# Three RMS norms taken off the matmuls' path: six units multiply unnormalised tiles and are scaled in the bank

## The reference, cut to what matters

```python
def rms_norm(x, g):
    return x * lax.rsqrt(jnp.mean(x * x, axis=-1, keepdims=True) + RMS_EPS) * g

def first_block(x, ...):
    h = rms_norm(x, norm_mix_g)
    qa, ka, va, qc, kc, vc, rx, rgate, gates = split(h @ w_in)
    ya = moba_attention(qa, ka, va)                 # 8 heads, softmax
    yb = rg_lru(causal_dwconv(rx, ...)) * gelu(rgate)   # a linear recurrence over the tokens
    yc = diff_attention(qc, kc, vc)                 # 4 heads, each with two softmaxes, then an RMS norm
    x = x + merge(ya, yb, yc, gates) @ w_out
    h = rms_norm(x, norm_ffn_g)
    u = causal_dwconv(h @ ffn_up)                   # 3 taps along the tokens
    x = x + (gelu(u_gate) * u_val) @ ffn_down
    return rms_norm(x, final_norm_g)
# then twice: proj = x @ w_in_2, three mixers, merge, w_o, layer norm, feed-forward, layer norm
```

## Time and profile before

| | |
|---|---|
| median of 3 runs | 1250.18 us (1248.51 to 1251.1) |
| the profiled execution | 1248.09 us, of which its span (first to last instruction) 1246.3 us |
| granted TensorE clock, mean | 0.992 |
| PE busy | 1220.6 us (98%) |
| DVE, ACT, POOL busy | 851.9, 709.0, 400.8 us |
| DMA | 212.70 MB, mean 171 GB/s |

### The profile page before, as it was taken

How to read it: one execution, slowest core, us unless ns; L and a number is a source line. 1 busy time by engine, 2 the same in 40 slices (tenths; PEclk the granted TensorE clock), 3 DMA queues, 4 the chain that set the end, 5 groups by cost and what they waited for, 6 DMA issues and landing times. The chain is left out here.

```text
span 1246.3 us, 27229 instructions
## 1 busy us (share of the span) xinstructions
PE 1220.6 (98%) x10224; PEld 1196.0 (96%) x10224; DVE 851.9 (68%) x1458; ACT 709.0 (57%) x1229; POOL 400.8 (32%) x376
## 2 busy tenths in 40 slices
PE   8999989999999999999999999999999999999997
PEld 8998989999999999998999999999999999999997
DVE  6857664576877764767668777755767667777755
ACT  5676675445766654466455566644466445666642
POOL 3006231023343412120338434413610338443313
PEclk9999989999999999999999999999999999999999
DMA  7654435555566666454654666565454654666662
GB/s 255 184 159 133 150 109 160 181 183 184 153 189 191 191 190 202 144 163 143 182 169 134 187 186 194 173 197 161 153 159 146 185 169 131 186 191 186 187 197 90
DMA packets 60288, 212.70 MB, mean 171 GB/s; under 512 B 6688, under 2 KB 7968, under 8 KB 60064
## 3 DMA queue, kind: packets, MB, share of 16 engines
q1 hardware_dynamic: 60192, 211.39, 55.9%
HBM read 210.31 MB, written 1.05 MB: 170 GB/s over the span
## 5 line engine op out<-in xcount | busy, mean ns | idle before, releaser
L1372 DVE TENSOR_TENSOR wlo<-raw,whi 128x1024 fp32r<-128x1024 f32 (+1 forms) x400 | 493.6, 1235 | 307.7 <-ACT whi L716 304.7
L1048 PE MATMUL bank<-xhi,whi 128*128 128x256 f32 x2240 | 638.3, 285 | 4.4 <-DVE wlo L1372 2.1
L1049 PE MATMUL bank<-xlo,whi 128*128 128x256 f32 x2240 | 625.6, 279 | 0.0
L1050 PE MATMUL bank<-xhi,wlo 128*128 128x256 f32 x2240 | 625.6, 279 | 0.0
L716 ACT ACTIVATE whi<-raw 128x1024 fp32r<-128x1024 f32 (+1 forms) x400 | 415.7, 1040 | 153.3 <-PE bank L1050 144.2
L1048 PEld LDWEIGHTS bank<-xhi,whi 128*128 128x128 f32 x2240 | 424.4, 189 | 15.3 <-issue 7.2
L1049 PEld LDWEIGHTS bank<-xlo,whi 128*128 128x128 f32 x2240 | 423.0, 189 | 0.6
L1050 PEld LDWEIGHTS bank<-xhi,wlo 128*128 128x128 f32 x2240 | 422.1, 188 | 0.0
L617 POOL TENSOR_TENSOR fprod<-ugate,uval 128x256 f32<-128x256 f32 x66 | 94.4, 1431 | 211.6 <-DVE uval L1717 206.0
L1048 PE MATMUL bank<-fhi,whi 128*128 128x256 f32 x528 | 147.4, 279 | 0.0
L1050 PE MATMUL bank<-fhi,wlo 128*128 128x256 f32 x528 | 147.0, 278 | 0.0
(11 more groups left out here) (201 smaller groups left out, 1294.0 us busy)
## 6 DMA issues: line engine op xcount, KB each, us to landing
raw<-in_w_win SPq DMA_DIRECT2D x140, 512.0 KB, 3.6
raw<-in_w_up SPq DMA_DIRECT2D x132, 512.0 KB, 3.6
raw<-in_w_down SPq DMA_DIRECT2D x48, 448.0 KB, 3.6
raw<-in_w_merge SPq DMA_DIRECT2D x32, 512.0 KB, 4.1
raw<-in_w_out SPq DMA_DIRECT2D x24, 512.0 KB, 3.5
raw<-in_w_down SPq DMA_DIRECT2D x24, 512.0 KB, 3.6
x<-in_x SPq DMA_DIRECT2D x4, 256.0 KB, 4.1
rgw<-in_rg_w SPq DMA_DIRECT2D x1, 1024.0 KB, 10.2
```

The costliest lines, as they stand in the source:

```text
L1048: pe.matmul(ps, whi[:, slot, w], hi, start=first, stop=False)
L1049: pe.matmul(ps, whi[:, slot, w], lo, start=False, stop=False)
L1050: return pe.matmul(ps, wlo[:, slot, w], hi, start=False, stop=last)
L1372: dve.tensor_tensor(wlo[:, n % RING, w], raw[:, n % RING, w], whi[:, n % RING, w].bitcast(f32), ALU.subtract) \
```

## The change

The three norms `mix` (ahead of `win1`), `ffn` (ahead of `up1`) and `final` (ahead of `win20`) are done otherwise. `x*g` is split into `raw_xhi` and `raw_xlo` (which lie in `yhi`, `ylo`) as each tile of `x` is made, and the first six units of the next stage (`RAW_UNITS`) multiply these; units 3 to 5 write to three spare banks. Sum, root and inverse run beside them; ACT copies the spread inverse to SBUF (`copy_inverse`), and DVE multiplies each of the six results by it in the bank (`scale_raw`) before anyone reads it. The normalised tiles, for unit 6 onwards, are made two at a time behind the results of units 0 to 3 (`normal`, `norm_hi`, `normal_low`), for `ffn` with the product by the inverse on POOL. The `ramp` and the `warm` matmuls of these norms go, but for 20 at the start. The first loads come in another order. In `win1` the six units come ahead of the recurrence's, and the steps get new unit numbers.

In the diff below, `load_pair` is the SP queue's; `normal` is the one on POOL; `copy_inverse`, the `hi_part` lines and `norm_hi` are ACT's; `raw_unit` and the wait for `LOW` (unit 6 of `up1`) are PE's; `scale_raw`, the `lo_part` lines, `invert` and `normal_low` are DVE's.

```diff
-PLAN1 = sum([[t, 24 + t] for t in range(KT)], []) + list(range(8, 24)) + list(range(32, WIN1))
+RAW_UNITS = 6
+PLAN1 = list(range(6)) + sum([[24 + t, 6 + t] for t in range(KT)], []) + list(range(14, 24)) + list(range(32, WIN1))
...
-        at(6 + 2 * t, "rg_gates", t)
-    at(22, "rg_roots",)
+        at(10 + 2 * t, "rg_gates", t)
+    at(25, "rg_roots",)
...
-    for pair in range(MOBA_H // 2):
-        at(23 + 3 * pair, "scores", pair)
+    for pair, n in enumerate((27, 30, 32, 34)):
+        at(n, "scores", pair)
         for i in range(2):
-            at(25 + 3 * pair + i, "weights", 2 * pair + i)
-        at(27 + 3 * pair, "values", 2 * pair)
+            at(n + 2 + i, "weights", 2 * pair + i)
+        at(n + 4, "values", 2 * pair)
     for h in range(DIFF_H):
-        at(35 + 3 * h, "scores", MOBA_H // 2 + h)
-        at(38 + 3 * h, "weights", MOBA_H + h)
-        at(39 + 3 * h, "values", MOBA_H + h)
-    at(41, "rg_gelu",)
-    at(49, "diff_sums",)
-    at(50, "diff_recip",)
+        at(36 + 2 * h, "scores", MOBA_H // 2 + h)
+        at(39 + 2 * h, "weights", MOBA_H + h)
+        at(40 + 2 * h, "values", MOBA_H + h)
+    at(46, "rg_gelu",)
+    at(48, "diff_sums",)
+    at(49, "diff_recip",)
     for h in range(DIFF_H):
-        at(51 + 2 * h, "diff_spread", h)
+        at(52 + 2 * h, "diff_spread", h)
...
+SPLIT_AHEAD = (0, 1, START["win20"])
...
+        SPARE = {RESULT[name] + i: (ps_score, ps_turn, ps_stat)[i - 3] for name in RAW_STAGE.values() for i in range(3, RAW_UNITS)}
+        inverse_rows = tmp[:, 2, :]
...
+            sp.dma_start(vec[:, 0:KT], args["vec"][:, 0:KT]).then_inc(load_gain, 16)
+            for i in (0, 1):
+                load_pair(i)
             load(0)
+            for i in (2, 3):
+                load_pair(i)
+            load(1)
...
+            def normal(which):
+                pool.wait_ge(inverse_copied, RAWI[which] + 1)
+                for t in range(KT):
+                    pool.tensor_tensor(dev[:, t, :], x[:, t, :], inverse_rows, ALU.mult).then_inc(normed_pool, 1)
...
+            def copy_inverse(which):
+                act.wait_ge(spread, SUM[which])
+                act.activation(inverse_rows, spread_inverse, ACT.Copy).then_inc(inverse_copied, 1)
...
+            hi_part(2)
+            hi_part(3)
             norm_root("mix", RMS_EPS)
-            hi_part(0)
-            norm_hi("mix", dev, {3: 1})
-            hi_part(2)
+            hi_part(4)
+            copy_inverse("mix")
...
+                    if raw_units(which, i, it):
+                        if 1 <= i <= RAW_UNITS - 2:
+                            hi_part(n + 3)
...
+                    if raw_units(which, i, it) and i:
+                        norm_hi(which, i - 1)
...
+            def raw_unit(which, i):
+                name = RAW_STAGE[which]
+                n, r = START[name] + i, RESULT[name] + i
+                sums = 1 if which == "mix" else 0
+                ready = [(raw_lo, KT * RAWI[which] + k + 1) for k in range(KT)] if i == 0 else None
+                plain(n, r, bank_of(r)[:, 0:S], ready=ready, split=(raw_xhi, raw_xlo),
+                      between=(lambda: rms_spread(which)) if which == "mix" and i == 2 else None)
+                if i == sums:
+                    rms_sums(which)
+                if i == 1 and which != "mix":
+                    rms_spread(which)
...
+                    if which in RAWI and i == 0:
+                        pe.wait_ge(*LOW[which, KT - 1])
...
+            def scale_raw(which, i):
+                n, ps = START[RAW_STAGE[which]] + i, bank_of(RESULT[RAW_STAGE[which]] + i)[:, 0:S]
+                if i == 0:
+                    dve.wait_ge(inverse_copied, RAWI[which] + 1)
+                dve.wait_ge(unit_done, n + 1)
+                dve.tensor_tensor(ps, ps, inverse_rows, ALU.mult).then_inc(raw_scaled, 1)
...
+                    if raw_units(which, i, it):
+                        if i == 0:
+                            lo_part(n + 2)
+                            invert(which)
+                            lo_part(n + 3)
+                        elif i <= RAW_UNITS - 2:
+                            lo_part(n + 3)
+                        scale_raw(which, i)
...
+                    if raw_units(which, i, it):
+                        normal_low(which, i - 1)
```

More of the change, by code:

```diff
@@ L418, in build, with bank_of, raw_units @@
             results(f"down2{l}", KT, res_new)
-        def bank_of(r):
+        RAW_STAGE = {"mix": "win1", "ffn": "up1", "final": "win20"}
+        GAIN = {"mix": "norm_mix_g", "ffn": "norm_ffn_g", "final": "final_g"}
+        RAWI = {n: i for i, n in enumerate(RAW_STAGE)}
+        SPARE = {RESULT[name] + i: (ps_score, ps_turn, ps_stat)[i - 3] for name in RAW_STAGE.values() for i in range(3, RAW_UNITS)}
+        raw_xhi, raw_xlo = yhi[:, 0:KT, :], ylo[:, 0:KT, :]
+        inverse_rows = tmp[:, 2, :]
+        def bank_of(r, it=0):
+            if isinstance(it, int) and r in SPARE:
+                return SPARE[r]
             return unit_bank[r % 3]
+        def raw_units(which, i, it=0):
+            return which in RAWI and i < RAW_UNITS and isinstance(it, int)
         def down_bank(name, t):
@@ L751, in norm_shift, with norm_hi @@
                         .then_inc(normed_act if last else x_hi, 1)
-            def norm_hi(which, src, after={}):
-                for t in range(KT):
-                    if t in after:
-                        hi_part(after[t])
+            def norm_hi(which, i):
+                src = x if which == "final" else dev
+                for t in ((2 * i, 2 * i + 1) if i < KT // 2 else ()):
                     act.wait_ge(*NORMED[which, t])
-                    act.activation(xhi[:, t, :], src[:, t, :], ACT.Copy).then_inc(x_hi, 1)
+                    if which == "ffn":
+                        act.activation(xhi[:, t, :], src[:, t, :], ACT.Copy, scale=col(GAIN[which], t)).then_inc(x_hi, 1)
+                    else:
+                        act.activation(xhi[:, t, :], src[:, t, :], ACT.Copy).then_inc(x_hi, 1)
@@ L883, in steps @@
                     STEPS[name](*a)
-                if n < last:
+                if n < last and n not in SPLIT_AHEAD:
                     hi_part(n + 3)
@@ L908, in _ @@
                 steps(n, WIN1 - 1)
+                norm_hi("mix", n)
             def merged_hi(base, t):
@@ L952, in wout @@
                     for u in due:
+                        if which not in LNI:
+                            raw_high(which, u)
                         square(which, u)
+                if which not in LNI:
+                    raw_high(which, KT - 1)
                 square(which, KT - 1)
@@ L1026, in _ @@
                     steps(n, first + MIX2)
+                    if l == 0:
+                        norm_hi("final", p)
                     if waiting is not None:
@@ L1084, in ramp, with plain @@
                         mm.then_inc(unit_done, 1)
-            def plain(n, result, ps, it=0, per=0, rper=0, ready=None, split=(xhi, xlo)):
+            def plain(n, result, ps, it=0, per=0, rper=0, ready=None, split=(xhi, xlo), between=None):
                 hi, lo = split
@@ L1091, in plain @@
                         pe.wait_ge(*ready[k])
+                    if between is not None and k == KT // 2:
+                        between()
                     mm = product_of(ps, n % RING, k, hi[:, k, :], lo[:, k, :], k == 0, k == KT - 1)
@@ L1740, in body @@
                         residual(name, t, n, alpha, down_bank(name, t), it, 6, 2)
+                    if which not in LNI and i % 3 == 1 and not (isinstance(it, int) and i < 3):
+                        raw_low(which, t - 1, it)
                 repeat(dve, name, DOWN, 6, body, peel_first=True)
```

274 lines of the change are left out of this document (163 added, 111 removed).

## The result

The changed kernel is slower: 1261.24 us, the median of 5 runs (1257.96 to 1262.64), against 1249.88 us of before on the same chip; ratio 1.0080, 95% interval 1.0063 to 1.0096. The forecast was 1246.1 us, in a range of 1239.5 to 1253: its sign and its range were both wrong. The profiled execution took 1261.24 us, its span 1259.5.

What follows compares the result with a forecast made beforehand. The prediction took PE, busy for 98% of the span, as the bound. Its terms, 1.5 - 10.5 + 9.1 - 4.2, gave -4.1 us, taken off the median of 1250.18: 1246.1 us, range 1239.5 to 1253.

Steps and rivals of the forecast that it cites:

- Term 1: Start of `win1`: PE waits 4 us in unit 2 for the inverse and the clock falls; +1.5 us.
- Term 2: Rest of `win1`: new slots remove the 3.86 us wait, its clock loss and other waits; -10.5 us.
- Rival (c): `win1`: dense pairs make one wait of some 3 us, so gains cancel; 1249.6 us, band 1247.7 to 1252.7, chance 0.23.
- Rival (d): Dense attention part of `win1`: a wait over 3 us brings the clock down; 1253.4 us, chance 0.15.
- Term 3: `ffn` norm in `up1`: a chain over ACT and DVE of 4.3 us a unit delays unit 6; +9.1 us.
- Term 4: `final` norm in `win20`: unit 6 starts earlier, DVE's work hidden by 1 us; -4.2 us.

Runs made afterwards that it cites:

- steps_only: The kernel before, norms as before, with only the changed kernel's order of units and step slots in `win1`: 1246.03 us, ratio 0.9964 to before.
- values_later: steps_only with the differential heads' values steps, sums and reciprocal one unit later: 1247.18 us, ratio 0.9961 to before.
- three_units: steps_only with the differential heads three units apart instead of two, and what follows them later: 1247.72 us, ratio 0.9973 to before.
- final_as_before: The changed kernel with the `final` norm done as before, `mix` and `ffn` raw, changed slots kept: 1256.55 us, ratio 1.0052 to before.
- final_repaired: The changed kernel with sines ahead of the first `raw_high` in `down1`, and rope and turn steps of `win20` three units later: 1259.83 us, ratio 1.0046 to before.
- after_again: The changed kernel, unedited, run and profiled once more: 1259.63 us.
- root_first: The changed kernel with ACT's root of `mix` ahead of unit 3's split and DVE's inverse ahead of its second half: 1260.59 us, ratio 1.0078 to before.
- scale_first: The changed kernel with DVE's scaling of a result ahead of the low split in units 1 to 4 of `up1`: 1257.59 us, ratio 1.0042 to before.
- all_repaired: The changed kernel with the edits of root_first and scale_first, and the sines edit of final_repaired: 1256.09 us, ratio 1.0034 to before.
- ffn_as_before: The changed kernel with the `ffn` norm done as before, `mix` and `final` raw, changed slots kept: 1252.58 us, ratio 1.0016 to before.
- mix_only: The changed kernel with `ffn` and `final` done as before, `mix` raw, all changed slots kept: 1250.43 us, ratio 0.9997 to before.

## Why the prediction was wrong

**Term 1, the start (+1.5): right in its mechanism, its size in part by luck.** The root stood behind the split of unit 3, PE waited 4.08 us in unit 2 (forecast 4), and unit 6 starts at 35.78 against 34.30: +1.48. The parts were a little off and cancelled: unit 3's weights landed at 21.1, not 19.3, so the wait ended at 24.1, not 22.3; and the clock took 1.7 us, not the 3.4 charged (half is granted for 3.4 us behind this wait). Nor is +1.48 the same in every execution. In the seven profiles with this start unedited unit 6 begins at 33.78 to 35.89, on average 35.15. In the five with the old start it begins at 33.39 to 34.55, on average 34.14. In the two earliest of the seven the weights landed near the forecast's 19.3, the wait was 2.10 and 2.28 us, the clock stayed at 1.00, and the start cost nothing. The forecast had that landing together with a wait of 4 us, and no profile shows the two together.

**Term 2, the rest of `win1` (-10.5): this step failed, by 5.6 us.** Unit 6 to `merge1` became 4.9 us shorter in the changed kernel and 5.4 in steps_only. The 3.86, its clock loss of 3.4 and the 1.69 did go, as the term said. But "the denser pairs leave DVE about 7 us of work in 8.5" counted DVE's work and not the order: a head's exponentials on ACT wait for DVE's logits, those stand behind a low split, and the turned weights are copied behind the exponentials. Two units have no room for that loop; three have. In the changed kernel the four waits of 158 to 181 take 3.5 of the missing 5.6 us, the new one at 133.12 takes 0.7, and the first two gave back 0.6 instead of 1.5. Rival (c), "the dense pairs make one wait of some 3 us", had the mechanism, with 3.6 us between 156 and 180 in steps_only. values_later (no gain) and three_units (gone) show that it is the rhythm and not one slot. Rival (d) asked for one dense wait of over 3.5 us; the longest was 1.04, and the clock did not fall there.

**Term 3, `ffn` (+9.1): mechanism right, size 1.5 too high.** The round is 4.26 us (forecast 4.3), and unit 6 starts 5.9 us later than before when both are counted from the last tile of `wout1` (forecast 5.65). The forecast took 0.118 us between matmuls "throughout" and so 329.75 as the old start of unit 6. The trace of before has 0.113 in `up1`, and 329.41. The clock's part was mis-sized: 1.9 us instead of 3.4. The windows of the changed kernel:

```profile
324.00:326.00 2.00, 0.00 (x0) 0.00 (x0) 1.26 (x4) 1.80 (x5) 0.06 (x1) 0.86 0.48 106
...
330.00:332.00 2.00, 0.13 (x1) 0.13 (x1) 1.93 (x5) 0.83 (x3) 0.00 (x0) 0.50 0.67 248
332.00:334.00 2.00, 2.00 (x10) 2.00 (x11) 1.11 (x3) 1.82 (x3) 0.25 (x1) 0.50 0.01 2
334.00:336.00 2.00, 2.00 (x12) 2.00 (x12) 1.56 (x1) 0.00 (x0) 2.00 (x2) 0.58 0.00 0
```

The clock was at half already while PE stood still, and half a clock costs only from 331.87, when PE goes on: 0.13 x 0.5 + 2 x 0.50 + 2 x 0.42 = 1.9 us. In the earlier trace rows it fell just as PE began again, so all of it was paid.

**Term 4, `final` (-4.2): this step failed, by 4.65 us.** Unit 6 of `win20` starts 21.4 us behind unit 0, where the forecast had 19.2: the wait of 2.61 us, at the turn step behind unit 4, stands in between. Counted from the end of `down1` unit 6 still gains 2.3 us. The 0.73 behind it and the 0.95 at the first `weights` step give back 1.7, and the stretch as a whole is 0.45 us longer. Of the last 1.1 us 0.45 are a rope step that now stands behind unit 6, as the forecast said; the rest has no wait of its own. "DVE ... hidden by 1 us" looked at the splits and the normalised tiles alone. A turn or rope step of PE needs the bank that DVE's share of the step before frees, and that share stood behind all the raw work: DVE was busy for 9.86 of the 10 us from 510. final_as_before shows that the 2.61 and 0.73 belong to the raw work, and final_repaired that moving the steps moves the waits. The gain of 2.3 is also the better of two cases. After waits of 2.61 to 2.73 us at this place half a clock followed for 3.4 us in four profiles (after_again, root_first, scale_first, all_repaired), where unit 6 gains 0.8 to 0.9 us; in those of the changed kernel and ffn_as_before it did not. The 0.95 is not the raw norm's: it comes with the later rope steps, which the forecast put at nothing.

**What the sum left out: this failed too.** The raw high parts in `down1` were costed as hidden for `ffn` and not looked at for `final`: 1.90 us. The later rope steps of `win21` were not looked at either: 0.9 us, of which PE's wait of 1.03 shows the place. The rest of the difference between the two profiles, some 5.7 us in `down1`, `up21`, `down21` and smaller pieces, has no wait to it; it goes with the matmuls' spacing (below). For the medians the steps add up as ratios: the slots of `win1` 0.9964, raw `mix` with the later rope steps 0.9997, raw `final` 1.0016, raw `ffn` 1.0080, that is -4.5, +4.1, +2.4 and +8.0 us, each uncertain by some 2 us. Of the +4.1 the traces give 1.6 to the raw start and 2.4 to the rope steps.

**What stays open.** The rope steps' price is read from the traces of kernels that differ in other things as well; an edit of these slots alone was not run. The raw `final` costs 1.9 to 2.1 us in `down1`, 2.4 by ffn_as_before against mix_only, and 3.5 by final_as_before against after. And the two layers behind the first tile of `wout20` take 583.3 to 586.2 us in the five profiles with all norms as before and the old rope slots (mean 585.1), and 585.5 to 588.9 in the nine others (mean 587.3). Of these 2.2 us 0.9 are the later rope steps of `win21`; for the other 1.3 I have no cause.

## What to carry to other kernels

Follow a loop over two engines in program order before believing that work is hidden: an engine that is busy for 7 of 8.5 us can still be late in each round. When work is put on an engine in one stage, look at every other step whose share on that engine frees a buffer, and at the stage ahead in which the new work is prepared. When a step moves, look at what it now stands ahead of: one rope step a unit later cost about 1 us in each layer. And undo a change part by part, every part of it: here the slots of `win1` alone, a little spread, gave 0.7%, while the rest cost 1.2%, some 0.2% of it for rope steps that none of the runs that undid a norm had put back.

## What the runs showed of the hardware

Matmuls of the same form have two spacings at a granted clock of 1.00: 24 of them take 2.72 or 2.83 us, 113 or 118 ns each. The level holds for tens of us and belongs to the execution. Windows of 40 us in `down21`, of before, then of after; both PE always busy:

```profile
1190.00:1230.00 40.00, 40.00 (x356) 40.00 (x354) 22.07 (x28) 17.14 (x22) 10.41 (x11) 1.00 0.57 167
```

```profile
1190.00:1230.00 40.00, 40.00 (x340) 39.95 (x339) 21.48 (x26) 16.27 (x20) 6.64 (x6) 1.00 0.65 184
```

Of fourteen profiles only that of before has the short spacing in most of `down21` (52.74 us against 54.7 to 54.85), so this profile flatters before. Its cause is open. The Trainium skill, "TensorE: Matmul & The Clock Gate", section "Wait — 56ns, not 53.3ns?", gives one start-to-start time for back-to-back matmuls at full clock, the columns at 2.4 GHz and about 2.5 ns more, which is 109 ns here as an estimate. Both levels lie above it, by 4 and by 9 ns, in a stream where each matmul has a weight load of its own.

POOL next to DVE, in the changed kernel, as in the earlier trace rows:

```profile
326.81 0.90 POOL L627 TENSOR_TENSOR flo<-fprod,fhi 128x256 fp32r<-128x256 f32 x1
```

```profile
327.05 1.74 DVE L1460 TENSOR_TENSOR wlo<-raw,whi 128x1024 fp32r<-128x1024 f32 x1
```

The split took 1.74 us instead of 1.21, 0.53 more, as in the earlier trace rows. It began when POOL's instruction had 0.66 us left, and it was not held for a whole one of 0.90; so the longer wait that the rule in the Trainium skill, "SBUF — State Buffer", section "SBUF: two separate sides", allows did not show here.
